# Storing a diffusion backbone's weight tiles in interleaved pairs, so that each array load reads 128 columns 8 bytes apart

## What is computed

```
z = u @ w_in                                   # layer 0: 21 column blocks of 128, plus 8 blocks for the values
y = concat(gla(z), mlstm(z)) @ w_out           # layer 0 mixer, 8 column blocks
q, k, v = heads(u @ w_qkv)                     # layer 1: 16 column blocks, 8 blocks for the values
y = softmax(q k' + bias) v @ w_out             # layer 1 mixer, 8 column blocks
a, g = split(u @ w_up, 2)                      # each layer: 2 x 22 column blocks (D_FF = 2816)
out = (gelu(conv3(a)) * g) @ w_down            # each layer: 22 blocks of 128 rows
```

## Time and profile before

| | |
|---|---|
| median of 3 runs | 1783.16 us |
| lowest and highest run | 1775.05 and 1783.86 us |
| profiled execution, its own time | 1782.06 us |
| span of that execution | 1780.2 us |
| mean granted TensorE clock | 0.984 |
| TensorE matmuls | 1709.4 us busy, 9744 instructions |
| TensorE weight loads | 1484.1 us busy, 9744 instructions |
| VectorE, ScalarE, GpSimd | 924.7, 755.4 and 543.3 us busy |
| read from HBM | 180.40 MB |

### The profile page before, as it was taken

The page is one execution under the profiler, slowest core; times in us unless marked ns, Lnnn a source line. Parts: engine busy times, 40 slices in busy tenths (PEclk is TensorE's granted clock), DMA queues, the critical chain, the costliest instruction groups (busy, mean ns, idle before and its releaser), DMA issues.

```text
span 1780.2 us, 26540 instructions
## 1 busy us (share of the span) xinstructions
PE 1709.4 (96%) x9744; PEld 1484.1 (83%) x9744; DVE 924.7 (52%) x1468; ACT 755.4 (42%) x1208; POOL 543.3 (31%) x249
## 2 busy tenths in 40 slices
PE   5999899997999999999999999999999899999997
PEld 2777788896899999999988888997668888888876
DVE  5777966667956566566523365001774532222344
ACT  3563434776332332323333445212884443334442
POOL 1122113553222332233222323322004234444442
PEclk9999999998999999999999999999999999999998
DMA  8323223443432433433321122121322123222221
GB/s 335 138 95 119 73 72 100 138 132 130 142 119 96 141 130 107 142 121 116 100 67 60 60 72 84 60 95 59 105 74 83 60 82 96 95 95 96 94 95 59
DMA packets 66588, 184.08 MB, mean 103 GB/s; under 512 B 5920, under 2 KB 26784, under 8 KB 65200
## 3 DMA queue, kind: packets, MB, share of 16 engines
q1 hardware_dynamic: 44784, 164.69, 27.4%
q10 hardware_dynamic: 21696, 17.88, 3.4%
HBM read 180.40 MB, written 2.15 MB: 103 GB/s over the span
## 4 chain that ended last, share of the span: by engine, by line
PE 80%; DVE 5%; ACT 2%; issue 1%; POOL 0%; ACTq 0%; DVEq 0%; POOLq 0%
PE ps L2363 28%; PE ps L2789 13%; PE ps L2362 13%; PE ps L2376 4%; PE ps L2443 3%; PE ps L2786 3%; PE ps L2721 2%; PE ps L2923 2%; PE ps L2902 2%; PE ps L2936 2%; PE ps L2449 1%; PE ps L2346 1%; PE ps L2456 1%; PE ps L2345 1%; PE ps L2636 1%
## 5 line engine op out<-in xcount | busy, mean ns | idle before, releaser
L692 POOL TENSOR_TENSOR wsp<-raw,wsp 128x1024 fp32r<-128x1024 f32 x185 | 457.0, 2470 | 1133.5 <-ACT wsp L763 1133.1
L763 ACT ACTIVATE wsp<-raw 128x1024 fp32r<-128x1024 f32 x185 | 196.3, 1061 | 453.1 <-PE ps L2363 350.5
L2362 PE MATMUL ps<-v_a,wsp 128*128 128x384 f32 x1008 | 342.7, 340 | 0.0
L2363 PE MATMUL ps<-v_b,wsp 128*128 128x386 f32 x1008 | 340.2, 337 | 0.0
L2789 PE MATMUL ps<-hsp,wsp 128*128 128x512 f32 x984 | 277.4, 393 | 2.5 <-DVE hsp L2009 2.5
L2789 PEld LDWEIGHTS ps<-hsp,wsp 128*128 128x128 f32 x984 | 183.6, 188 | 45.3 <-issue 4.4
L2363 PE MATMUL ps<-uf,wsp 128*128 128x512 f32 x888 | 201.4, 389 | 0.0
L2363 PEld LDWEIGHTS ps<-uf,wsp 128*128 128x128 f32 x888 | 166.7, 188 | 34.6
L2363 PEld LDWEIGHTS ps<-v_b,wsp 128*128 128x128 f32 x1008 | 193.5, 192 | 0.0
L2362 PEld LDWEIGHTS ps<-v_a,wsp 128*128 128x128 f32 x1008 | 189.2, 188 | 0.0
L2026 DVE SCALAR_TENSOR_TENSOR conv<-apad,vec,conv 128x770 f32<-128x770 f32 (+1 forms) x44 | 47.6, 1082 | 204.2 <-ACT conv L1201 204.2
(11 more groups left out here) (320 smaller groups left out, 2537.2 us busy)
## 6 DMA issues: line engine op xcount, KB each, us to landing
raw<-in_weights SPq DMA_DIRECT2D x281, 512.0 KB, 3.8
nab<-in_nabias ACTq DMA_DIRECT2D x32, 256.0 KB, 3.0
start_w<-in_start SPq DMA_DIRECT2D x6, 1024.0 KB, 20.9
h<-in_x SPq DMA_DIRECT2D x4, 768.0 KB, 14.5
mD<-rows_scratch ACTq DMA_DIRECT2D x12, 256.0 KB, 4.1
mqs<-rows_scratch ACTq DMA_DIRECT2D x12, 256.0 KB, 5.3
h<-in_x ACTq DMA_DIRECT2D x2, 1536.0 KB, 6.4
start_w<-in_start SPq DMA_DIRECT2D x4, 512.0 KB, 12.5
```

Of the source, the lines that this page charges most:

```text
L692: pool.tensor_tensor(w[:, 1, :], raw[:, raw_index(s) % 4, :], w[:, 0, :].bitcast(F32), ALU.subtract)\
L763: act.activation(split_of(s)[:, 0, :], raw[:, raw_s % 4, :], ACT.Copy).then_inc(*own.one(hi_ready))
L2362: pe.matmul(cx, w, x_cx[:, k, xp, :], start=first, stop=last)
L2363: mm = pe.matmul(lat, w, x_lat[:, k, xp, :], start=first, stop=last)
```

## The change

Two tiles that stood one behind the other in a block, 128 columns each, now share 256 columns: column `c` of the first is at place `2 c`, column `c` of the second at `2 c + 1`. The host writes them so (`in_pairs`), for every block of `column_blocks` and for the two `w_down` matrices, not for the value blocks, which are streamed. Every place that loads a weight tile takes it with `weights_of(s, wp, k)`: 128 columns with a step of two elements, 8 bytes. Before, the step was 4 bytes. The number, order, engines and waits of all instructions are the same, and so are the DMA sizes, the memory map, and what ScalarE and GpSimd do with a block, since they treat all 1024 columns alike.

```diff
@@ -487,6 +487,11 @@
+        def weights_of(s, wp, k):
+
+            pair = split_of(s)[:, wp, 2 * P * (k // 2):2 * P * (k // 2) + 2 * P]
+            return pair.rearrange("p (c t) -> p c t", t=2)[:, :, k % 2]
@@ -2356,7 +2361,7 @@
-                        w = split_of(s)[:, wp, tile(k)]
+                        w = weights_of(s, wp, k)
@@ -2440,20 +2445,20 @@
-                    mm = pe.matmul(ps[:, n % 2, :], wsp[:, s % 2, wp, tile(k)], u[:, k, xp, LAT], start=first, stop=last,
+                    mm = pe.matmul(ps[:, n % 2, :], weights_of(s, wp, k), u[:, k, xp, LAT], start=first, stop=last,
...
@@ -2780,7 +2785,7 @@
-                        w = split_of(s_down + b)[:, wp, 512 * kk + P * mm_:512 * kk + P * mm_ + P]
+                        w = weights_of(s_down + b, wp, 4 * kk + mm_)
...
@@ -3038,7 +3043,13 @@
 def column_blocks(w):
 
     m = w.shape[1] // P
-    return w.reshape(KT, P, m, P).transpose(2, 1, 0, 3).reshape(m, P, BLOCK)
+    return in_pairs(w.reshape(KT, P, m, P).transpose(2, 1, 0, 3).reshape(m, P, BLOCK))
+
+
+def in_pairs(blocks):
+
+    n = blocks.shape[0]
+    return blocks.reshape(n, P, KT // 2, 2, P).transpose(0, 1, 2, 4, 3).reshape(n, P, BLOCK)
@@ -3075,9 +3086,9 @@
-    stream += [up(g["ffn_w_up"][0]), row_blocks(g["ffn_w_down"][0])]
+    stream += [up(g["ffn_w_up"][0]), in_pairs(row_blocks(g["ffn_w_down"][0]))]
...
-    stream += [up(g["ffn_w_up"][1]), row_blocks(g["ffn_w_down"][1])]
+    stream += [up(g["ffn_w_up"][1]), in_pairs(row_blocks(g["ffn_w_down"][1]))]
```

More of the change, by code:

```diff
@@ L2342, in two_blocks @@
                         for a, (wp, xp) in enumerate(PASSES):
-                            w, first, last = split_of(s + b)[:, wp, tile(k)], k == 0 and a == 0, k == KT - 1 and a == 2
+                            w, first, last = weights_of(s + b, wp, k), k == 0 and a == 0, k == KT - 1 and a == 2
                             if cx is not None:
@@ L2448, in project @@
                             pe.wait_ge(cx_took.sem, n)
-                        mm = pe.matmul(ps[:, 2, 0:N_CTX], wsp[:, s % 2, wp, tile(c)], u[:, c, xp, CTX],
+                        mm = pe.matmul(ps[:, 2, 0:N_CTX], weights_of(s, wp, c), u[:, c, xp, CTX],
                                        start=(c == 0 and a == 0), stop=False, skip_group_check=True)
@@ L2455, in project @@
                         for a, (wp, xp) in enumerate(PASSES):
-                            mm = pe.matmul(ps[:, 2, 0:N_CTX], wsp[:, s % 2, wp, tile(c)], u[:, c, xp, CTX], start=False,
+                            mm = pe.matmul(ps[:, 2, 0:N_CTX], weights_of(s, wp, c), u[:, c, xp, CTX], start=False,
                                            stop=(c == KT - 1 and a == 2), skip_group_check=True)
@@ L2655, in out_first @@
                     for a, (wp, xp) in enumerate(PASSES):
-                        w = wsp[:, s % 2, wp, tile(k)]
+                        w = weights_of(s, wp, k)
                         first, last = k == 0 and a == 0, k == KT - 1 and a == 2
@@ L2720, in half_product @@
                 for a, (wp, xp) in enumerate(PASSES):
-                    mm = pe.matmul(out, split_of(s)[:, wp, tile(k)], x[:, k, xp, in_lat(t)], start=(k == 0 and a == 0),
+                    mm = pe.matmul(out, weights_of(s, wp, k), x[:, k, xp, in_lat(t)], start=(k == 0 and a == 0),
                                    stop=(k == KT - 1 and a == 2), skip_group_check=True)
@@ L2845, in late_context @@
                             for wp, xp in PASSES:
-                                mm = pe.matmul(ctx_of(mm_), split_of(s_down + b)[:, wp, 512 * kk + P * mm_:512 * kk + P * mm_ + P],
+                                mm = pe.matmul(ctx_of(mm_), weights_of(s_down + b, wp, 4 * kk + mm_),
                                                hcx[:, 2 * (b - FT + N_LATE) + kk, xp, :], start=False,
@@ L2947, in out_last @@
                     for a, (wp, xp) in enumerate(PASSES):
-                        mm = pe.matmul(ps[:, m, :], wsp[:, s % 2, wp, tile(k)], uy[:, k, xp, :], start=(k == 0 and a == 0),
+                        mm = pe.matmul(ps[:, m, :], weights_of(s, wp, k), uy[:, k, xp, :], start=(k == 0 and a == 0),
                                        stop=(k == KT - 1 and a == 2), skip_group_check=True)
```

## The result

The changed kernel takes 1795.6 us (median of 14 runs, 1787.9 to 1800.33) against 1784.48 us of the kernel before in the same measurements (14 runs, 1775.05 to 1789.46). The ratio is 1.0071, with a 95% interval of 1.0052 to 1.0089: slower by 11 to 13 us, beyond the 0.5% that can be told from no change. Forecast were 1705 us and a range that ended at 1790.

The account below looks back on a forecast made before the run. The prediction took TensorE's matmuls as the bound. It summed 88.8 - 3.2 (256-column limit) - 7.5 (stretches mixed with the heads) - 1 (half clock) = 77 us off 1782.06, giving 1705 us; range 1685 to 1790.

Parts of the forecast that it names:

- What bounds the kernel: Whole kernel: TensorE hardly waits, so time is the number of matmuls times what each takes; matmuls recorded for 96% of the span.
- The surcharge and where it is absent: Time of a full-clock float32r matmul beyond its columns, 13.3 to 17 ns; about 2.5 with plain float32, none at half clock.
- What load and stream do to each other: At 7104 changed matmuls: a full-speed stream overtakes the load's walk through memory; 8-byte steps equalize them, surcharge falls to 2.5 ns.
- equal pace: Plain float32 and half-clock streams walk 4 bytes per 0.83 ns, like the load's 4 per 0.8, so they have little or no surcharge.
- spare supply: Rival: a half-speed stream has reserve to cover a pause between instructions, a full-speed one has none; 1783 us, chance 0.18.
- 7104 x (15 - 2.5) = 88.8 us: Main gain: 7104 matmuls with changed loads each drop from a mean surcharge of 15 ns to 2.5 ns.
- The lesser term: Weight loads of 128 columns keep their own speed with an 8-byte step, still recorded with 188 ns.
- the bubble of fixed size: Rival: a fixed pause at each full-speed stream's start, which the load's layout can't touch; 1783 us, chance 0.18.
- The toll per piece: Rival: the stream pays for each piece of memory the load opens, twice as many now; 95 us more, 1878, chance 0.15.
- the slow load: Rival: loads 8 bytes apart run at half speed per column; 264 us more, 2046 us, chance 0.05.

Follow-up runs that it names:

- the isolated runs: Kernels that only issue matmuls, one kind in a row, none of the reference's work; 512 columns with loads 4 and 8 bytes apart took 228.3 and 233.3 ns in the first.

## Why the prediction was wrong

*What bounds the kernel*: right. TensorE's dense runs set the time before and after, and three runs of 512-column matmuls alone (936, 288 and 192 of them) give 9.4 of the 11 to 13 us lost.

*The surcharge and where it is absent*: the readings were right, and the isolated runs repeat them (13 ns at 256 and 512 columns, 2.5 with plain float32).

*"What load and stream do to each other"* is the step that failed. I took absence in the earlier trace rows for a matter of equal pace. But in both the stream also walks at half its speed. The prediction named that reading, spare supply, under its rivals and gave it 0.18. The runs decide for the supply, though not for a pause of fixed size: with a load that reads one element, walking at no pace at all, the 512-column matmul still has a surcharge of 17.6 ns, while a stream that reads one element has 5.4. The 12.5 ns a matmul that were to go weren't the load's to give back. At 256 columns, where it saves 5 ns, at most a part was. Of the term 7104 x (15 - 2.5) = 88.8 us nothing came: the 936-matmul run, which should have taken 202 us, took 218.41, six matmuls of the earlier trace rows took 1.06 us and not 0.98, and the 256-column run kept its 120 ns a matmul. The lesser term, that the load's own speed doesn't change, was nearly right (194 ns, 188 named).

*The rival that lay nearest*, the bubble of fixed size at 1783 us, had no cost for the change, and is not right either: bfloat16 doesn't have the 13 ns, and the load does set the rhythm. What I had not among the cases at all is the one that came: the sum of load and stream falls into a rhythm that depends on starts, steps and widths, the kernel's 512-column runs had the best one that any run with an ordinary stream showed, some 226.7 ns, and the change put them into one of 233.3. Its price could have been bounded from the earlier trace rows, whose surcharges of 16 and 17 ns show what a less fortunate mixture costs: 3 to 4 ns more on the some 1800 matmuls of the 512-column runs is 5 to 7 us, and the swing up to 27 ns in the earlier trace rows was a warning that it can be more.

*The toll per piece and the slow load* are refuted at 8 bytes, in the kernel by the 17.29 us of the 256-column run. They were the only cases that named a slower kernel, together with 0.20, but at prices of 95 and 264 us; neither is what came. The slow load is real beyond that, at 12 and 16 bytes.

*The two rules of the Trainium skill.* The one of "TensorE: Matmul & The Clock Gate", section "Step-by-step: what each phase is for", that loading the next tile steals nothing from the running matmul, fits most of the missing gain, but not the 5 ns that a one-element load saves at 256 columns, and not the loss: no rule of independent ports makes the same stream take 233.3 ns in place of 226.7 when the load starts 64 bytes further on. The one of "Advanced Engine Details and Errata", section "SBUF Cachelines", on lines of 16 bytes with two hits each, agrees with the load's own speed, which holds at 4 and 8 bytes and drops at 12; but at 12 and 16 bytes the recorded lengths differ (252 and 311 ns) though both steps leave fewer than two hits on most lines, and a stream 8 bytes apart, which has two hits a line like the load, takes 453.8 ns in place of 226.9.

*What stays open*: by what rule load and stream fall into their rhythm. Distances often differ by multiples of 3.3 ns (226.7, 230.2 and 233.3), the one-element load makes 512 columns slower and 256 faster, a stream moved by 64 bytes costs less than a load moved by 64, and the same stage took 233.3 or 235.6 ns in two kernels that differ only in layer 0. I have no account that gives all of these. What is shown is that the step of 8 bytes puts the 512-column runs from 226.7 to 233.3 ns, and that a move of 64 bytes without the step does the same; why is not shown.

## What to carry to other kernels

Where a cost is absent in a case that differs in two things, here equal pace and spare supply, price the change by both readings before choosing; one kernel of bare matmuls, with the load or the stream held on one element, would have told them apart. A dense run of equal matmuls can stand in a rhythm that depends on where its operands begin: measure the distance of starts per width, and treat a move of a buffer by 64 bytes as a change that needs a measurement. Look at the order of widths too; three of one and three of the other gained about 0.3% here (0.14 to 0.5) for nothing.

## What the runs showed that I had not expected

- Moving one buffer by 64 bytes costs this kernel 0.77% (0.56 to 0.98).
- A float32r stream whose columns lie 8 bytes apart takes twice as long, 453.8 ns for 512 columns in place of 226.9, while a load with the same step keeps its pace.
- With loads of only 32 columns, 512-column matmuls are not faster but 4 to 5 ns slower than in the settled rhythm of full loads (231 against 227 ns).
- Identical instructions in layer 1 ran at 233.3 or 235.6 ns a matmul in two kernels that differ only in layer 0, one profiled execution each.
